# Recurrent layer of a two-model transformer kernel: output projection by tiles of the recurrence over eight sums in four PSUM banks, decay straight from the exponential, and the projection's weight splits moved behind the gates

## The chip, the cores and the metric

One core of a Trainium2 chip runs the whole kernel as one program. The metric is the device time of one execution in microseconds. Engines: TensorE (PE, with its weight loads PEld), VectorE (DVE), ScalarE (ACT), GpSimd (POOL), and SyncE (SP), which here only issues the weight transfers.

## What is computed

The first model is two layers of mixed attention over 256 tokens with 256 context tokens; its output goes through the second model: a recurrent layer, an MLP, a shared key/value projection, chunked attention and a second MLP. The change lies in the recurrent layer (width 1408 = 11 blocks of 128, model width 1024 = 8 blocks):

```python
z = hn @ w_in
gate, xr = jnp.split(z, 2, axis=-1)
xr = causal_depthwise_conv(xr, conv_w, conv_b)
r = jax.nn.sigmoid(xb @ w_a + b_a)            # by groups of 88 channels
i = jax.nn.sigmoid(xb @ w_x + b_x)
log_a = (-LRU_C * r) * jax.nn.softplus(-lam)
a = jnp.exp(log_a)
u = jnp.sqrt(-jnp.expm1(2.0 * log_a)) * (i * x)
h = scan(a, u)                                # h[t] = a[t] * h[t-1] + u[t]
x = x + gate_mod * ((h * jax.nn.gelu(gate)) @ w_out)
```

Behind it stands the norm of the MLP: the mean of the squares of x over the 1024 channels.

## The kernel before

**Numbers and layout.** All matrices are fp32, multiplied as three fp32r products of a high and a low part (`three`, lines 1678 to 1681: high by high, high by low, low by high). Activations lie with channels on the partitions and tokens in the columns.

**Units.** The weights come in 204 units, in a fixed order (`UNITS`, `PROGRAM`). Every engine walks through the same list of steps. For unit i, SyncE loads the raw weights into one of four slots (a slot is free when the unit four loads before has been split), ScalarE makes the high part (`split_hi`, L733), VectorE the low part (`split_lo`, L1054), and TensorE multiplies. As a rule both halves of unit i + 2 are made at the step of unit i, ahead of that unit's own evacuation (`evac`). The high part waits for the unit three before, whose slot it takes. For five units, `POOL_SPLIT` (63, 101, 125, 157, 173), POOL makes the low part instead (L703), because VectorE is then busy with a norm.

**The recurrent layer** is made of units 100 to 123:
- 100 to 110, `lin`: the input projection, one block of gate and of xr each. Output: `GT` (gelu of the gate) and `XR` (after the convolution).
- 111 to 116, `lgate`: the two gate matrices for two blocks each (the last for one). ScalarE evacuates: tanh of half of r (L850) and of i (L853), then `LA` = tanh of half the negative log of the decay (L859), then the decay as exponential (L863) into `T`. VectorE computes s = (a + 1) * tanh = 1 - a (L1299), bounds it (L1300), writes a = 1 - s into `LA` (L1301), and makes (i + 1) * x in `LU` (L1302) and s * (s - 2) in `XR` (L1303).
- the step `lscan`: ScalarE takes the square roots in four pieces (L1009), blocks [0, 1], [2..5], [6..9] and [10] (`LSTEPS`); VectorE multiplies a piece (L1596) and scans it block by block (L1599); POOL multiplies each scanned block by the gate (L715), which gives y; ScalarE makes the high part of y (L1012), VectorE the low part (`scan_lo`, L1492), which it does two blocks behind the scan.
- 117 to 119, `lpart`: TensorE adds blocks [0..3], [4..7] and [8..10] of y (`LPARTS`) to the four output chunks 0 to 3, which lie in two PSUM banks. Six warm-up matmuls (L1652) come first, as soon as the first block has been scanned.
- 120 to 123, `lout`: output chunks 4 to 7, one by one, each over all eleven blocks.

The high halves of units 117 and 118 stand on ScalarE ahead of the evacuations of the last two gate units, the low halves likewise on VectorE; those of 119 stand inside `lscan`.

**The norm behind it.** VectorE adds each projected chunk to x (`residual`, L1238), ScalarE squares it (L746), POOL adds the squares of chunks 1 to 6 onto that of chunk 0 one after the other (`add_squares`, L681); TensorE sums the result and the square of chunk 7 over the partitions (`sumsq`, L1900), with two warm-up matmuls behind each of the two; ScalarE takes the root, TensorE spreads it (L1909), and VectorE begins the norm's product (L1559). POOL adds the squares of unit i - 1 at the step of unit i, and its own split of unit i + 2 comes behind that:

```python
if i and fed_norm(UNITS[i - 1]) is not None:
    add_squares(UNITS[i - 1])
if i + 2 in POOL_SPLIT:
    pool.wait_ge(*at("hi", w))
    pool.tensor_tensor(wslot(wlo, w, size), ...)
```

How many chunks POOL adds is fixed by the norm, and the sum on TensorE waits for the last of them:

```python
def added(n):
    return 6 if n in (1, 3, 8) else 7
# sumsq, first part
pe.wait_ge(*at("sqadd", (n, added(n) - 1)))
```

The norm here is number 5; number 8, in the last layer, is fed by `out` units of two chunks each.

## Time and profile before

| | us |
|---|---|
| median of three runs | 1732.64 |
| the three runs | 1732.54, 1732.64, 1736.28 |
| span of the profiled execution | 1730.9 |
| time of the profiled execution as a run | not given on the page |
| TensorE busy | 1658.9 (96%) |
| VectorE busy | 1302.2 (75%) |
| ScalarE busy | 819.2 (47%) |
| POOL busy | 243.0 (14%) |

The span is from the first to the last instruction of one profiled execution. Busy times of different engines overlap. A matmul's duration is longer than the distance to the next, since matmuls are pipelined; the distance is what a matmul costs. "PEclk" is the clock granted to TensorE as a share of 2.4 GHz: 1.00 is that level, 0.50 is 1.2 GHz.

### The profile page before, as it was taken

How to read it: one execution, taken by the hardware profiler on the slowest of the kernel's cores; microseconds unless marked ns; L12 is line 12 of the kernel's file. 1: busy time of each engine (PE TensorE's matmuls, PEld its weight loads, DVE VectorE, ACT ScalarE, POOL GpSimd, SP SyncE). 2: the span in 40 equal slices, each digit the busy share in tenths (PEclk: the TensorE clock that was granted, in tenths of full speed). 3: DMA queues.
4: the chain of work that ended last, by engine and by line, in shares of the span. 5: the costliest groups of instructions: out<-in, count | busy, mean ns of one | idle time of the engine just before them, and what ended most of it. 6: DMA issues, size and time to landing. Idle time of an engine off the chain costs nothing.

```text
span 1730.9 us, 28129 instructions
## 1 busy us (share of the span) xinstructions
PE 1658.9 (96%) x11542; PEld 1464.1 (85%) x11542; DVE 1302.2 (75%) x1818; ACT 819.2 (47%) x1186; POOL 243.0 (14%) x199
## 2 busy tenths in 40 slices
PE   6999989999999999999999999969999999899999
PEld 3887768788788777986999999959999999699887
DVE  5687863887988878857578777797988868758574
ACT  3433752543133323646554546575635444555352
POOL 0423001011001111540310121013000220030000
PEclk8999999999999999999999999989999999999999
DMA  8644002243565458320347566635998966137552
GB/s 345 254 150 167 2 26 73 98 146 116 192 240 219 178 193 307 122 74 1 122 158 277 196 218 239 212 123 172 358 365 321 342 219 223 46 125 277 183 173 95
DMA packets 46575, 317.83 MB, mean 184 GB/s; under 512 B 5232, under 2 KB 6256, under 8 KB 12272
## 3 DMA queue, kind: packets, MB, share of 16 engines
q1 hardware_dynamic: 45936, 312.68, 50.0%
q0 software_dynamic: 512, 3.35, 0.5%
q8 instruction: 92, 1.51, 0.4%
q14 instruction: 35, 0.29, 0.0%
HBM read 314.96 MB, written 1.05 MB: 183 GB/s over the span
## 4 chain that ended last, share of the span: by engine, by line
PE 80%; DVE 11%; ACT 3%; issue 3%; POOL 2%; DMA 1%; SPq 0%; DVEq 0%; ACTq 0%
PE PM L1679 20%; PE PM L1680 19%; PE PM L1681 19%; PE PM L1833 5%; PE PM L1835 3%; PE PM L1963 2%; DVE wlo L1054 2%; PE PX L1999 1%; DVE acc L1088 1%; PE PX L1872 1%; PE PO L2025 1%; PE PX L1652 1%; DMA raw<-in_ada 1%; PE PO L2014 1%; PE PX L1929 1%
## 5 line engine op out<-in xcount | busy, mean ns | idle before, releaser
L1054 DVE TENSOR_TENSOR wlo<-raw,whi 128x2048 fp32r<-128x2048 f32 (+2 forms) x199 | 437.8, 2200 | 73.1 <-ACT whi L733 72.6
L1679 PE MATMUL PM<-H,whi 128*128 128x256 f32 (+1 forms) x1526 | 480.2, 315 | 7.7 <-DVE H L1480 3.0
L1680 PE MATMUL PM<-H,whi 128*128 128x256 f32 (+1 forms) x1526 | 476.2, 312 | 0.0
L1681 PE MATMUL PM<-H,wlo 128*128 128x256 f32 (+1 forms) x1526 | 476.1, 312 | 0.0
L733 ACT ACTIVATE whi<-raw 128x2048 fp32r<-128x2048 f32 (+3 forms) x204 | 365.5, 1792 | 143.2 <-PE PM L1681 48.7
L1679 PEld LDWEIGHTS PM<-H,whi 128*128 128x128 f32 x1526 | 291.1, 191 | 32.1 <-issue 7.9
L1681 PEld LDWEIGHTS PM<-H,wlo 128*128 128x128 f32 x1526 | 291.1, 191 | 16.5
L1680 PEld LDWEIGHTS PM<-H,whi 128*128 128x128 f32 x1526 | 291.3, 191 | 15.9
L1088 DVE SCALAR_TENSOR_TENSOR acc<-raw,silc,acc 128x512 f32<-128x512 f32 x328 | 245.1, 806 | 5.3 <-DMA raw<-in_ada 4.2
L1679 PE MATMUL PM<-G,whi 128*128 128x256 f32 (+1 forms) x608 | 192.7, 317 | 1.7 <-DVE X L1238 1.6
L1680 PE MATMUL PM<-G,whi 128*128 128x256 f32 (+1 forms) x608 | 190.8, 314 | 0.0
L1681 PE MATMUL PM<-G,wlo 128*128 128x256 f32 (+1 forms) x608 | 190.7, 314 | 0.0
L681 POOL TENSOR_TENSOR T<-T 128x256 f32<-128x256 f32 (+1 forms) x39 | 63.5, 1628 | 509.4 <-ACT T L746 508.8
L1679 PE MATMUL PM<-whi,H 128*128 128x256 f32 x464 | 133.2, 287 | 0.0
L1680 PE MATMUL PM<-wlo,H 128*128 128x256 f32 x464 | 131.3, 283 | 0.0
L1681 PE MATMUL PM<-whi,H 128*128 128x256 f32 x464 | 131.3, 283 | 0.0
L1679 PEld LDWEIGHTS PM<-G,whi 128*128 128x128 f32 x608 | 115.8, 191 | 13.1 <-issue 6.1
L1681 PEld LDWEIGHTS PM<-G,wlo 128*128 128x128 f32 x608 | 115.9, 191 | 7.0
L1680 PEld LDWEIGHTS PM<-G,whi 128*128 128x128 f32 x608 | 115.9, 191 | 6.6
L1238 DVE SCALAR_TENSOR_TENSOR X<-PM,mod,X 128x256 f32<-128x256 f32 x120 | 54.5, 481 | 83.5 <-issue 47.3
L622 POOL TENSOR_TENSOR T<-T 128x512 f32<-128x512 f32 (+1 forms) x44 | 48.3, 1098 | 453.9 <-DVE T L1276 453.9
L827 ACT ACTIVATE T<-PM,feat 128x512 f32<-128x512 f32 (+1 forms) x88 | 54.3, 668 | 117.1 <-PE PM L1681 108.3
(243 smaller groups left out, 2675.4 us busy)
## 6 DMA issues: line engine op xcount, KB each, us to landing
raw<-in_ada SPq DMA_DIRECT2D x104, 1024.0 KB, 5.2
raw<-in_wm SPq DMA_DIRECT2D x93, 1024.0 KB, 5.1
raw<-in_wl SPq DMA_DIRECT2D x68, 1024.0 KB, 5.1
raw<-in_wl SPq DMA_DIRECT2D x32, 704.0 KB, 4.3
raw<-in_wm SPq DMA_DIRECT2D x5, 768.0 KB, 4.5
raw<-in_wm SPq DMA_DIRECT2D x4, 704.0 KB, 4.1
X<-in_x SPq DMA_DIRECT2D x1, 2048.0 KB, 12.2
bias<-in_bias POOLq DMA_DIRECT2D x1, 2048.0 KB, 11.0
```

Of the source, the lines that this page charges most:

```text
L622: pool.tensor_tensor(g, g, val, ALU.mult).then_inc(*tick("prod", i))
L681: pool.tensor_tensor(sqslot(n, 0, W), sqslot(n, 0, W), sqslot(n, k, W), ALU.add).then_inc(*tick("sqadd", (n, k)))
L733: act.activation(wslot(whi, i, usize(u)), slot_raw(RAW_AT["w", i], usize(u)), ACT.Copy)\
L827: act.activation(dst, pm(i, part * 512, W), ACT.Identity, scale=fcol("cw", (l * 3 + 1) * 44 + n), bias=fcol("cb", l * 44 + n)).then_inc(*t ...
L1054: dve.tensor_tensor(wslot(wlo, i, usize(u)), slot_raw(n, usize(u)), wslot(whi, i, usize(u)).bitcast(F32), ALU.subtract)\
L1088: ins = dve.scalar_tensor_tensor(out=dst, in0=w, scalar=s, in1=dst, op0=ALU.mult, op1=ALU.add)
L1238: ins = dve.scalar_tensor_tensor(out=dst, in0=pm(i, m * each + who * 256, 256), scalar=modc(v, who, c), in1=dst, op0=ALU.mult, op1=ALU.add)
L1679: pe.matmul(out, st_hi, mv_hi, start=first, stop=False)
L1680: pe.matmul(out, st_hi, mv_lo, start=False, stop=False)
L1681: return pe.matmul(out, st_lo, mv_hi, start=False, stop=last)
L1833: pe.matmul(pm(i, c * 512, 512), wslot(whi, i, 128, w0), mh[:, k * 512:k * 512 + 512], start=(k == 0), stop=False)
L1835: ins = pe.matmul(pm(i, c * 512, 256), wslot(wlo, i, 128, w0), mh[:, k * S:k * S + 256], start=False, stop=(k == kt - 1))
```

## The change

1. The projection. `lpart` units 117 to 119 now hold two blocks of y each, [0, 1], [2, 3], [4, 5], for all eight output chunks; the eight sums lie in four PSUM banks (`lsum`). Units 120 to 123 are now `lend`: blocks 6 to 10 for two output chunks each. Each `lend` unit feeds the norm with two chunks.
2. The decay. ScalarE writes the exponential straight into `LA` and the tanh into `T`; VectorE's instruction that wrote 1 - s into `LA` is gone.
3. The splits. Unit 117 is split behind the evacuation of the fifth gate unit, 118 no longer at the sixth but in `lscan` behind block 1, 119 behind block 3 and 120 behind block 6.
4. The scan. Its pieces are [0], [1, 2], [3..6], [7..10], and the low part of y is made one block behind the scan, not two.

```diff
-LPARTS = [[0, 1, 2, 3], [4, 5, 6, 7], [8, 9, 10]]
-LSTEPS = [[0, 1], [2, 3, 4, 5], [6, 7, 8, 9], [10]]
+LPARTS = [[0, 1], [2, 3], [4, 5]]
+LEND = [6, 7, 8, 9, 10]
+LSTEPS = [[0], [1, 2], [3, 4, 5, 6], [7, 8, 9, 10]]
...
-        add("lpart", "M0", n, len(ks), 512, 256)
-    for n in range(4, KD):
-        add("lout", "M0", n, NL, 128, 256)
+        add("lpart", "M0", n, len(ks), 1024, 256)
+    for n in range(KD // 2):
+        add("lend", "M0", n, len(LEND), 256, 256)
...
 def chunks_of(u):
 
-    if u["kind"] == "out":
+    if u["kind"] in ("out", "lend"):
         return [2 * u["idx"], 2 * u["idx"] + 1]
...
+        def lsum(c):
+
+            return PM[:, c // 4, c % 4 * 256:c % 4 * 256 + 256]
+
+        def lsplit_at(u):
+
+            if u["kind"] == "lgate" and u["idx"] >= len(GATE_UNITS) - 2:
+                return "late" if u["idx"] == len(GATE_UNITS) - 2 else None
+            return None if u["kind"] == "lpart" and u["idx"] < 2 else "first"
+
+        LSPLIT = {1: first_of("lpart", "M0") + 1, 3: first_of("lpart", "M0") + 2, 6: first_of("lend", "M0")}
...
-                        ins = act.activation(LA[:, j * 256:j * 256 + 256], rs[:, c * 256:c * 256 + 256], ACT.Tanh, scale=lcol(6, j), bias=lcol(6, j))
+                        ins = act.activation(LA[:, j * 256:j * 256 + 256], rs[:, c * 256:c * 256 + 256], ACT.Exp, scale=lcol(7, j), bias=lcol(7, j))
...
-                        ins = act.activation(rs[:, c * 256:c * 256 + 256], rs[:, c * 256:c * 256 + 256], ACT.Exp, scale=lcol(7, j), bias=lcol(7, j))
+                        ins = act.activation(rs[:, c * 256:c * 256 + 256], rs[:, c * 256:c * 256 + 256], ACT.Tanh, scale=lcol(6, j), bias=lcol(6, j))
...
-                        if j == 2:
-                            split_hi(first_of("lpart", "M0") + 2)
+                        if j in LSPLIT:
+                            split_hi(LSPLIT[j])
...
-                    dve.tensor_scalar(th, s, -1.0, 1.0, ALU.mult, ALU.add).then_inc(*C.link("dve_chain"))
...
-                            if j >= 2:
-                                scan_lo(j - 2)
-                            if j == 5:
-                                split_lo(first_of("lpart", "M0") + 2)
-                    scan_lo(NL - 2)
+                            if j >= 1:
+                                scan_lo(j - 1)
+                            if j - 1 in LSPLIT:
+                                split_lo(LSPLIT[j - 1])
...
-                        for c in range(4):
-                            w0 = m * 512 + c * 128
-                            ins = three(pm(first_of("lpart", "M0"), c * 256, 256), wslot(whi, i, 128, w0), wslot(wlo, i, 128, w0),
-                                        mh[:, k * 256:k * 256 + 256], ml[:, k * 256:k * 256 + 256], k == 0 and c % 2 == 0, k == NL - 1 and c % 2 == 1)
+                        for c in range(KD):
+                            w0 = m * 1024 + c * 128
+                            ins = three(lsum(c), wslot(whi, i, 128, w0), wslot(wlo, i, 128, w0),
+                                        mh[:, k * 256:k * 256 + 256], ml[:, k * 256:k * 256 + 256], k == 0 and c % 2 == 0, False)
+                elif kind == "lend":
+                    for c in range(2):
+                        for m, k in enumerate(LEND):
+                            if c == 0:
+                                pe.wait_ge(*at("hlo", ("y", k)))
+                            w0 = m * 256 + c * 128
+                            ins = three(lsum(2 * u["idx"] + c), wslot(whi, i, 128, w0), wslot(wlo, i, 128, w0),
+                                        mh[:, k * 256:k * 256 + 256], ml[:, k * 256:k * 256 + 256], False, k == NL - 1 and c == 1)
```

`added` and `POOL_SPLIT` are as before. How the instructions stand on three engines (each row: line, operation, output and inputs, shape, the semaphores that it waits for, and how often in a row):

POOL, from the gate multiplications of the scan to the norm behind the projection and on. Before:

```order
L715 TENSOR_TENSOR LU<-XR,GT 128x256 [waits s_lh] x11
L681 TENSOR_TENSOR T<-T 128x256 [waits s_sq]
L681 TENSOR_TENSOR T<-T 128x256 [waits s_sq,s_sqadd] x5
L703 TENSOR_TENSOR wlo<-raw,whi 128x2048 [waits s_hi]
L681 TENSOR_TENSOR T<-T 128x256 [waits s_sq]
```

Now:

```order
L724 TENSOR_TENSOR LU<-XR,GT 128x256 [waits s_lh] x11
L690 TENSOR_TENSOR T<-T 128x256 [waits s_sq]
L690 TENSOR_TENSOR T<-T 128x256 [waits s_sq,s_sqadd] x4
L712 TENSOR_TENSOR wlo<-raw,whi 128x2048 [waits s_hi]
L690 TENSOR_TENSOR T<-T 128x256 [waits s_sq,s_sqadd]
```

The addition of chunk 6 stood ahead of the split of unit 125 and stands behind it now.

ScalarE, from the end of the fifth gate unit (111 + 4) to the roots. Before:

```order
L863 ACTIVATE T<-T,lk 128x256 [waits s_act_chain]
L863 ACTIVATE T<-T,lk 128x256
L733 ACTIVATE whi<-raw 128x2048 [waits s_unit,s_raw2]
L850 ACTIVATE T<-PM,lk 128x256 [waits s_la,s_prep,s_unit,s_hi]
L853 ACTIVATE LU<-PM,lk 128x256
L859 ACTIVATE LA<-T,lk 128x256 [waits s_pm_act]
L863 ACTIVATE T<-T,lk 128x256 [waits s_act_chain]
L1009 ACT_TABLE_LOAD
L1009 ACTIVATE XR<-XR 128x512 [waits s_la]
L1009 ACTIVATE XR<-XR 128x1024 [waits s_la] x2
```

Now:

```order
L872 ACTIVATE T<-T,lk 128x256 [waits s_act_chain]
L872 ACTIVATE T<-T,lk 128x256
L742 ACTIVATE whi<-raw 128x2048 [waits s_unit,s_raw1]
L859 ACTIVATE T<-PM,lk 128x256 [waits s_la,s_prep,s_unit,s_hi]
L862 ACTIVATE LU<-PM,lk 128x256
L868 ACTIVATE LA<-T,lk 128x256 [waits s_pm_act]
L872 ACTIVATE T<-T,lk 128x256 [waits s_act_chain]
L1018 ACT_TABLE_LOAD
L1018 ACTIVATE XR<-XR 128x256 [waits s_la]
L1018 ACTIVATE XR<-XR 128x512 [waits s_la]
L1018 ACTIVATE XR<-XR 128x1024 [waits s_la] x2
```

The split that stands between the two gate units is now that of 117 (slot raw1), which stood one unit further ahead; that of 118 (raw2) is gone from here.

VectorE, in the scan, from the multiplication of the second piece. Before:

```order
L1596 TENSOR_TENSOR LU<-LU,XR 128x1024 [waits s_ls]
L1599 SCALAR_TENSOR_TENSOR XR<-LA,LU 128x256 [waits s_dve_chain]
L1492 TENSOR_TENSOR H_54<-LU,H_54 128x256 [waits s_hhi]
L1599 SCALAR_TENSOR_TENSOR XR<-LA,LU 128x256
L1492 TENSOR_TENSOR H_54<-LU,H_54 128x256 [waits s_hhi]
```

Now:

```order
L1606 TENSOR_TENSOR LU<-LU,XR 128x512 [waits s_ls]
L1609 SCALAR_TENSOR_TENSOR XR<-LA,LU 128x256 [waits s_dve_chain]
L1502 TENSOR_TENSOR H_54<-LU,H_54 128x256 [waits s_hhi]
L1609 SCALAR_TENSOR_TENSOR XR<-LA,LU 128x256
L1502 TENSOR_TENSOR H_54<-LU,H_54 128x256 [waits s_hhi]
L1065 TENSOR_TENSOR wlo<-raw,whi 128x2048 [waits s_hi]
L1606 TENSOR_TENSOR LU<-LU,XR 128x1024 [waits s_ls]
```

A split of 2048 columns, waiting for ScalarE's half, has come in between the second piece and the third; a second one stands after two more blocks, and one of 1280 columns after block 7.

## Rows read from the trace of the kernel before

**Rows 1.** The page: parts 1 and 6, TensorE's share, and the transfers of 1024 KB.

```profile
PE 1658.9 (96%) x11542; PEld 1464.1 (85%) x11542; DVE 1302.2 (75%) x1818; ACT 819.2 (47%) x1186; POOL 243.0 (14%) x199
...
raw<-in_wm SPq DMA_DIRECT2D x93, 1024.0 KB, 5.1
```

**Rows 2.** Time by stage: stretch, length, busy us of each engine (instructions), clock, DMA share, GB/s.

```profile
1141.00:1154.00 13.00, 0.39 (x4) 0.18 (x2) 12.10 (x19) 12.73 (x19) 0.00 (x0) 0.60 0.42 145
1154.00:1174.00 20.00, 18.36 (x115) 16.97 (x116) 19.79 (x25) 5.79 (x12) 10.15 (x11) 0.83 0.13 45
1174.00:1194.00 20.00, 20.00 (x169) 20.00 (x168) 12.70 (x14) 12.04 (x15) 8.72 (x7) 1.00 0.66 219
...
1205.00:1390.00 185.00, 184.70 (x1586) 179.69 (x1585) 160.10 (x194) 92.60 (x93) 12.36 (x6) 1.00 0.89 336
```

**Rows 3.** ScalarE in order of time: start us, us, what, shapes, count [idle before].

```profile
1140.13 1.90 ACT L733 ACTIVATE whi<-raw 128x2048 fp32r<-128x2048 f32 x1
1142.06 0.84 ACT L850 ACTIVATE T<-PM,lk 128x256 f32<-128x256 f32 x2
...
1144.78 1.09 ACT L863 ACTIVATE T<-T,lk 128x256 f32<-128x256 f32 x2
1145.78 1.89 ACT L733 ACTIVATE whi<-raw 128x2048 fp32r<-128x2048 f32 x1
```

**Rows 4.** VectorE in order of time, from the last split before the scan to its end.

```profile
1148.84 2.28 DVE L1054 TENSOR_TENSOR wlo<-raw,whi 128x2048 fp32r<-128x2048 f32 x1
...
1153.66 1.27 DVE L1599 TENSOR_TENSOR_SCAN XR<-LA,LU 128x256 f32<-128x256 f32 x2
...
1159.04 0.39 DVE L1492 TENSOR_TENSOR H<-LU,H 128x256 fp32r<-128x256 f32 x1
1159.35 1.21 DVE L1599 TENSOR_TENSOR_SCAN XR<-LA,LU 128x256 f32<-128x256 f32 x1
...
1162.27 2.29 DVE L1054 TENSOR_TENSOR wlo<-raw,whi 128x1536 fp32r<-128x1536 f32 x1
...
1174.10 0.42 DVE L1492 TENSOR_TENSOR H<-LU,H 128x256 fp32r<-128x256 f32 x1 [0.20 <-ACT H L1012]
```

**Rows 5.** POOL in order of time: one gate multiplication in the scan.

```profile
1159.19 0.82 POOL L715 TENSOR_TENSOR LU<-XR,GT 128x256 f32<-128x256 f32 x1 [0.63 <-DVE XR L1599]
```

**Rows 6.** TensorE in order of time: the warm-up at the scan, and the norm's sum.

```profile
1154.61 5.46 PE L1652 MATMUL PX<-cst 128*128 128x256 f32 x12 [13.22 <-DVE XR L1599]
1159.51 0.78 PE L1679 MATMUL PM<-H,whi 128*128 128x256 f32 x1
...
1193.41 0.51 PE L1900 MATMUL PO<-cst,T 128*128 128x2 f32 x4
1193.77 1.11 PE L1652 MATMUL PX<-cst 128*128 128x256 f32 x4
1194.72 0.54 PE L1900 MATMUL PO<-cst,T 128*128 128x2 f32 x4
```

**Rows 7.** VectorE: residual behind unit 122, and the first product of norm 5.

```profile
1189.70 0.48 DVE L1238 SCALAR_TENSOR_TENSOR X<-PM,mod,X 128x256 f32<-128x256 f32 x1 [1.94 <-issue]
...
1196.71 0.48 DVE L1559 SCALAR_TENSOR_TENSOR T<-X,mod,PO 128x256 f32<-128x256 f32 x1 [0.95 <-PE PO L1909]
```

**Rows 8.** VectorE's residual of two chunks in the last layer, then POOL's adds and split.

```profile
1532.74 0.88 DVE L1238 SCALAR_TENSOR_TENSOR X<-PM,mod,X 128x256 f32<-128x256 f32 x2 [2.69 <-issue]
...
1533.87 3.36 POOL L681 TENSOR_TENSOR T<-T 128x256 f32<-128x256 f32 x2 [2.40 <-ACT T L746]
1537.18 4.55 POOL L703 TENSOR_TENSOR wlo<-raw,whi 128x2048 fp32r<-128x2048 f32 x1
```

**Rows 9.** TensorE by the microsecond: stretch, length, busy us (instructions), granted clock, DMA share, GB/s.

```profile
1141.00:1142.00 1.00, 0.39 (x4) 1.00 0.80 298
...
1143.00:1144.00 1.00, 0.00 (x0) 0.83 0.03 11
1144.00:1145.00 1.00, 0.00 (x0) 0.50 0.00 0
```

More of the change, by code:

```diff
@@ L214, in fed_norm @@
     n = FEEDS.get((u["kind"], u["st"]))
-    if u["kind"] == "lpart" and u["idx"] < len(LPARTS) - 1:
-        return None
     if n is None or u["idx"] < FIRST_HALF.get(u["kind"], 0):
@@ L265 @@
 COLUMNS_AT = [ROWS_AT[i - 1] if i else [] for i in range(NU)]
-POOL_SPLIT = [u["i"] + 2 for u in UNITS if (fed_norm(u) or 0) >= 3 and chunks_of(u)[-1] == KD - 1 and u["kind"] != "lpart"]
+POOL_SPLIT = [u["i"] + 2 for u in UNITS if (fed_norm(u) or 0) >= 3 and chunks_of(u)[-1] == KD - 1]
 def raw_order():
@@ L1020, in _ @@
                         ffn_stage2(UNITS[i - 1])
-                    if (u["kind"], u["idx"]) != ("lpart", 0):
+                    if lsplit_at(u) == "first":
                         split_hi(i + 2)
@@ L1025, in _ @@
                     evac(u)
+                    if lsplit_at(u) == "late":
+                        split_hi(i + 2)
                     for hv in DIRECT_AT[i]:
@@ L1057, in chunk_soon @@
             def chunk_soon(u):
-                return (fed_norm(u) or 0) >= 3 and u["kind"] != "lpart" and (u["kind"] != "down" or u["idx"] % KD > 0)
+                return (fed_norm(u) or 0) >= 3 and (u["kind"] != "down" or u["idx"] % KD > 0)
             marks = [None, None]
@@ L1224, in residual @@
                 st = u["st"]
-                v = vec_base(st) + (2 if u["kind"] in ("out", "lout", "lpart") else 5)
+                v = vec_base(st) + (2 if u["kind"] in ("out", "lend") else 5)
                 n = fed_norm(u)
@@ L1230, in residual @@
                 cs = chunks_of(u)
-                each = 256 if u["kind"] == "lpart" else 512
                 for m, c in enumerate(cs):
@@ L1262, in evac @@
                     dve.tensor_tensor(v4, v4, r4, ALU.mult).then_inc(*tick("avn", i))
-                elif kind in ("out", "down", "lout", "w2") or (kind, u["idx"]) == ("lpart", len(LPARTS) - 1):
+                elif kind in ("out", "down", "lend", "w2"):
                     residual(u)
@@ L1609, in _ @@
                     soon = chunk_soon(u)
-                    if (u["kind"], u["idx"]) != ("lpart", 0) and not soon and not (u["kind"] == "w1" and wide(u)):
+                    if lsplit_at(u) == "first" and not soon and not (u["kind"] == "w1" and wide(u)):
                         split_lo(i + 2)
@@ L1616, in _ @@
                     evac(u)
-                    if soon:
+                    if soon or lsplit_at(u) == "late":
                         split_lo(i + 2)
@@ L1657, in pm_free @@
             def pm_free(i):
-                if i >= 2 and not (UNITS[i]["kind"] == "lpart" and UNITS[i]["idx"]):
+                if i >= 2 and UNITS[i]["kind"] != "lend" and not (UNITS[i]["kind"] == "lpart" and UNITS[i]["idx"]):
                     u = UNITS[i - 2]
@@ L1669, in pm_free @@
                         pe.wait_ge(*at("vcopy", i - 2))
-                    if u["kind"] in ("out", "down", "lout", "w2") or (u["kind"], u["idx"]) == ("lpart", len(LPARTS) - 1):
+                    if u["kind"] in ("out", "down", "lend", "w2"):
                         n = fed_norm(u)
@@ L1786, in unit @@
                 pm_free(i)
-                if kind == "lpart" or (kind == "lout" and UNITS[i - 1]["kind"] == "lpart"):
+                if (kind, u["idx"]) == ("lpart", 0):
                     pe.wait_ge(*at("pm_act", first_of("lpart", "M0") - 1))
```

15 lines of the change are left out of this document (7 added, 8 removed).

## The prediction

> **What bounds the kernel now.** I read the page's first part, then the time by stage, then each engine's instructions in the stretch that the change touches. TensorE is busy for 96% of the span [rows 1], so most stages end with its last matmul, and work taken off another engine is worth something only where TensorE waits for it. One such place lies in the recurrent layer. From 1141 to 1154 us TensorE is busy for 0.39 us of 13, while ScalarE and VectorE are busy for 12.73 and 12.10; right behind it, TensorE works at a mean granted clock of 0.83; from 1174 on it is busy without a gap at 20.00/169 = 0.12 us a matmul, and it stays so from 1205 to 1390 [rows 2]. So the stretch is: gates, decay and scan on ScalarE and VectorE, then the projection on TensorE, then the fifth norm, whose first matmul (the sum of squares) starts at 1193.41 and whose first product on VectorE starts at 1196.71 [rows 6, 7]. What comes later is bound by TensorE and passes on what it is given: in 185 us it has 0.3 us of idle time that could take up a shift. The sum is therefore the move of that 1196.71.
>
> **The gates and the decay.** ScalarE's order is split 117 (1.90 us), gate unit 4 (from 1142.06 to 1144.78 + 1.09 = 1145.87), split 118 (1.89), gate unit 5, table load, square roots [rows 3]. The change puts split 117 behind gate unit 4 and takes split 118 out of the stretch: the roots start 1.9 us earlier. VectorE loses its half of split 118 here (2.28 us [rows 4]), and the first multiplication ahead of the scan is of 256 columns, not 512: at 2.28/2048 columns that is 0.3 us. The instruction dropped per gate unit (1 - s) lies on VectorE in time that it mostly waits for ScalarE; swapping exponential and tanh costs ScalarE nothing, since one table load of each kind stays. I take 2.6 us in all: the first scan starts at 1153.66 - 2.6 = 1151.05.
>
> **The scan chain.** In the steady part VectorE and POOL take turns. The scan that is issued at 1159.35 ends at 1160.56, though a scan takes 0.6 us alone (two in 1.27); it ends 0.55 us after the POOL multiplication that ran from 1159.19 to 1160.01. The low part of y (1159.04 to 1159.43) does run under that POOL instruction, and a block costs 1.45 us [rows 4, 5]. The Trainium skill (SBUF - State Buffer, "SBUF: two separate sides") says that the shared port pair is held for the whole of an instruction and the loser fully blocks. By that the low part could not lie under it, a block would cost about 0.3 us more, ten of them 3 us, and the sum below would be 9.6 instead of 6.6; the row decides, for the same instructions.
>
> From first scan to last low part it is now 1153.66 to 1174.52, 20.9 us [rows 4]. The change takes out the split of 1536 columns (2.3) and puts in two of 2048 (2 x 2.28) and one of 1280 (1.4 by its columns, plus 0.6 behind a POOL instruction). VectorE has the first two at once behind a low part, but ScalarE makes their other half only behind its copy of the same y block: 0.42 + 1.90 from the end of POOL's product, against 0.55 + 0.3 for scan and low part, so VectorE waits some 1.4 us, twice. The last multiplication of 256 columns between blocks goes (0.9 with its wait for POOL). 20.9 - 2.3 + 4.6 + 2.0 + 2.8 - 0.9 = 27.1, and the last low part is done at 1151.05 + 27.1 = 1178.2, 3.6 us later than now.
>
> **The projection.** The 264 matmuls stay 264; before, 12 per block of y lie under the scan and 132 behind it, now 24 for each of the first six blocks and 120 in the four end units. The six warm-up matmuls start 0.95 us after the first scan and take 4.9 [rows 6]; useful work starts at 1156.9. With 0.7 lost on its first, slow matmuls, TensorE alone would be through at 1156.9 + 0.7 + 264 x 0.12 = 1189.3. But it comes to block 8 at 1175.6 and has to wait for blocks 9 and 10. The weights are the same 5632 KB in seven transfers; a slot is free for the next one when VectorE's split of the unit four loads before is done, so those of the last two end units are asked for at about 1159 and 1166, land in some 5 us [rows 1], and ScalarE wants them after 1179: no wait. Behind the last low part stand 3 + 15 + 90 = 108 matmuls: 1178.2 + 0.15 + 13.0 = 1191.35. Before, the last one gave way at 1193.41. This part gains 2.1 us.
>
> **The norm behind it, where I see the loss.** POOL executes in order. Before, chunk 6 was added at the step of its unit and POOL's own split of unit 125 came after it. Now chunks 6 and 7 come from one unit, POOL adds 4 and 5, splits unit 125, and only then adds 6; TensorE's first sum of squares waits for that addition, with the warm-up and everything of the norm queued behind it. The same order, adds 4 and 5 and then a split, is to be seen in the last layer: residual of two chunks at 1532.74, the adds held behind VectorE's split (3.36 us for two), POOL's split from 1537.18 for 4.55, so it is through 9.0 us after the residual began [rows 8]. Here that residual follows the third end unit at 1191.35 - 30 x 0.12 + 0.09 (as at 1189.70 now [rows 7]) = 1187.85. Split through at 1196.85, add 6 (0.82 [rows 5]) at 1197.65, sum of squares at 1197.75. TensorE is idle for 6.4 us. Against 1193.41 that is +4.3 us.
>
> **The clock.** When TensorE went idle at 1141.4 the granted clock was still 1.00 in the first microsecond, 0.83 in the third and 0.50, the 1.2 GHz level, from the fourth [rows 9]. A wait of 6.4 us is longer than that, so the norm's matmuls should run at 1.2 GHz. Price: four records of warm-up take 0.95 us at full clock (1193.77 to 1194.72), twelve took 4.90 at half, 0.24 and 0.41 each; eight of them 1.4 more. The small matmuls around them, 0.36 us ahead of the first warm-up and twice about as much later, 1.2 in all, at the same ratio of 1.7 give 0.9 more [rows 6]. Bounds: nothing, if the clock holds or comes back at once, and 3.3, if the whole of 1193.41 to 1196.71 doubles. I take 2.3, nearest to the rows.
>
> Sum: +4.3 + 2.3 = **+6.6 us**, in parts -2.1 (projection ends earlier), +6.4 (wait), +2.3 (clock). On the profiled execution the span goes from 1730.9 to 1737.5. The page gives no time of its own for that execution; the fastest run, 1732.54, is 1.6 us above the span and the median 0.1 above that. I add to the median: **1739.2 us**. Of the 4 us by which the third run stood higher nothing shows in the trace. A difference of 0.3%, 5.2 us, is about what a measurement can tell from none.
>
> **Rivals.**
> A, the clock holds through the wait: +4.3, 1736.9, which is not slower by 0.3%. For it: after 1141.4 it held for some 2 us. Against: it fell in that gap, the one long gap in these rows. It decides if TensorE waits hardly longer than those 2 us, or does something in between. 0.10.
> B, also not slower by 0.3%: the scan chain does not hold the projection. Place: VectorE's two waits for ScalarE's halves and block 10. If block 10 is done by 1176, the projection ends with TensorE at 1189.3, 2.1 us earlier, and the sum is +4.5, 1737.1. Against: two splits of 2.28 us stand in the chain whatever the waits are. 0.12.
> C, the addition is not late, so the change does not stall the norm: it needs POOL's split to be through when square 6 is, at 1192.4. Then 1191.35 + 0.1 + 0.5 + 0.5 + 0.8 + 0.1 = 1193.35 and the sum is -0.1, 1732.5. Against: the split takes 4.55 and its input, ScalarE's half, is not made before unit 122 ends. 0.08.
> D, four banks: each block of y goes round eight sums in four banks instead of four in two. If that pulled the clock to 1.2 GHz, 144 matmuls would cost 0.08 more each (ratio 1.7): 12, less the 2 us of slack, so +17, 1749. For the two banks of now the clock is 1.00 from 1174. 0.05. The Trainium skill (TensorE: Matmul & The Clock Gate, "A second HAM failure mode: psum-queue depth-cycling") tells of a kernel where cycling through banks made the clock oscillate; by that rule this case decides.
> E, faster by over 5.2 us: the whole bound of the gain is 4.1 us with no wait in the norm, so something outside the stretch would have to help. 0.05.
>
> **The numbers.** The forecast has 0.60, with a range of its own from +5.2 to +8.5 (a clock price between 1 and 3, the chain within 1 us). Faster by over 0.3%: E, 0.05. Within: A, B and C, 0.30. Slower: forecast and D, 0.65. The range goes from 1735.0 to 1742.5: it takes in the forecast, A and B with a microsecond or two of their spread and leaves out C, D and E, 0.18.
>
> **What would show it.** In the changed profile: first scan near 1151; two gaps of some 1.4 us on VectorE ahead of its splits in the scan; TensorE waiting for low parts near 1177; the last projection matmul near 1191; then a wait of TensorE of 6.4 us for POOL's addition, and a granted clock of 0.5 behind it. Wrong would be a first sum of squares before 1195, POOL's addition 6 ahead of its split, or an idle stretch in the norm stage with the clock still at 1.00.

## The result, and the profile of the changed kernel

The changed kernel is slower: its median of six runs is 1741.1 us (1739.24 to 1749.78) beside 1734.76 us of six runs of the kernel before (1732.54 to 1736.28). The ratio of the two is 1.0051, with a 95% interval from 1.0033 to 1.0070, so 0.3% to 0.7% slower, or 6 to 12 us. The profiled execution of the changed kernel has a span of 1737.4 us and was a run of 1739.24.

The span alone misleads here. It is 6.5 us longer than that of before, the medians stand 6.3 apart, and 6.6 was the forecast, but they agree by accident. To see it, follow one row that both kernels have: the reciprocal in norm 4, ahead of the recurrent layer (DVE, start, duration), first of the kernel before, then of the changed one.

```profile
1046.58 0.17 DVE L1537 RECIPROCAL rcol<-rcol 128x2 f32<-128x2 f32 x1 [1.44 <-ACT rcol L974]
```

```profile
1045.96 0.17 DVE L1547 RECIPROCAL rcol<-rcol 128x2 f32<-128x2 f32 x1 [1.62 <-ACT rcol L983]
```

The changed kernel comes 0.6 us early to the stretch. That is no work of the change: in the fourteen traces of this case the row stands anywhere from 1043.74 to 1052.47. Norm 5's first product starts at 1205.60 instead of 1196.71 [rows 7], 8.9 us later:

```profile
1205.60 0.87 DVE L1569 SCALAR_TENSOR_TENSOR T<-X,mod,PO 128x256 f32<-128x256 f32 x2 [2.31 <-PE PO L1926]
```

From norm 4's reciprocal to that product it is 159.64 us against 150.13: **the change costs 9.5 us**, and the missing 3 us of the span are 0.6 ahead of the stretch and 2.4 in the last MLP, which the last section shows. Comparisons of traces below use such distances within one trace, since whole executions of one kernel differ by more than the terms in question (the 29 to 34 runs of the kernel before in each of the three groups of experiments spread over 10 us and more).

Time by stage of the changed kernel, to be held against [rows 2] (stretch, length, then busy us of TensorE, its weight loads, VectorE, ScalarE and POOL with their instructions, granted clock, DMA share, GB/s):

```profile
1154.00:1174.00 20.00, 19.96 (x155) 19.37 (x155) 17.18 (x20) 7.31 (x10) 5.64 (x7) 0.97 0.23 70
1174.00:1194.00 20.00, 16.36 (x117) 15.55 (x116) 13.15 (x17) 11.46 (x16) 9.32 (x9) 0.91 0.61 213
1205.00:1390.00 185.00, 184.70 (x1572) 179.20 (x1572) 161.08 (x204) 94.06 (x98) 8.66 (x4) 1.00 0.85 325
```

TensorE is fed under the scan, from 1154 to 1174, as the change sets out to do: 155 matmuls instead of 115. Behind that it has gaps and a lower clock. What it waits for, from 1110 to 1215 us (sum, times, longest):

```profile
PE PX L1661 <- DVE XR L1609: 11.0, 1, 11.0
PE PO L1917 <- POOL T L690: 6.2, 1, 6.2
...
PE PM L1688 <- DVE H L1502: 2.6, 3, 0.9
```

The first wait is the one of 13.2 us ahead of the scan, now 2.2 shorter. The second is new: the norm's sum waits for POOL's addition. The third, three waits for low parts of y, was there in another form. VectorE in the scan (start, duration, idle before):

```profile
1150.46 0.69 DVE L1609 TENSOR_TENSOR_SCAN XR<-LA,LU 128x256 f32<-128x256 f32 x1
1151.07 0.67 DVE L1606 TENSOR_TENSOR LU<-LU,XR 128x512 f32<-128x512 f32 x1
...
1156.09 2.29 DVE L1065 TENSOR_TENSOR wlo<-raw,whi 128x2048 fp32r<-128x2048 f32 x1 [1.38 <-ACT whi L742]
...
1163.44 2.29 DVE L1065 TENSOR_TENSOR wlo<-raw,whi 128x2048 fp32r<-128x2048 f32 x1 [1.38 <-ACT whi L742]
...
1170.80 2.03 DVE L1065 TENSOR_TENSOR wlo<-raw,whi 128x1280 fp32r<-128x1280 f32 x1
...
1175.16 1.22 DVE L1609 TENSOR_TENSOR_SCAN XR<-LA,LU 128x256 f32<-128x256 f32 x1
...
1177.82 0.43 DVE L1502 TENSOR_TENSOR H<-LU,H 128x256 fp32r<-128x256 f32 x1 [1.07 <-ACT H L1021]
```

The two gaps of 1.38 us and the two long splits are as forecast. So is the third split's 2.03 (the same shape takes 1.49 at 1179.27, with nothing on POOL, so beginning under a POOL instruction cost 0.54). The gap of 1.07 ahead of the last low part, where 0.20 stood before [rows 4], was not. POOL and VectorE at the end of the projection:

```profile
1190.63 3.34 POOL L690 TENSOR_TENSOR T<-T 128x256 f32<-128x256 f32 x2 [1.03 <-ACT T L755]
1193.92 4.50 POOL L712 TENSOR_TENSOR wlo<-raw,whi 128x2048 fp32r<-128x2048 f32 x1
1198.38 0.73 POOL L690 TENSOR_TENSOR T<-T 128x256 f32<-128x256 f32 x1
```

```profile
1193.10 0.88 DVE L1249 SCALAR_TENSOR_TENSOR X<-PM,mod,X 128x256 f32<-128x256 f32 x2 [0.52 <-DVE wlo L1065]
```

Chunk 6 is ready for POOL from 1194 on and is added at 1198.38, behind the split. TensorE in the norm, against [rows 6]:

```profile
1199.25 0.99 PE L1917 MATMUL PO<-cst,T 128*128 128x2 f32 x4 [6.25 <-POOL T L690]
1200.10 2.05 PE L1661 MATMUL PX<-cst 128*128 128x256 f32 x4
1201.94 0.85 PE L1917 MATMUL PO<-cst,T 128*128 128x2 f32 x4
```

Last, TensorE by the microsecond (busy us, granted clock, DMA share, GB/s):

```profile
1176.00:1177.00 1.00, 0.20 (x1) 1.00 0.95 401
1177.00:1178.00 1.00, 0.41 (x3) 1.00 0.02 8
1178.00:1179.00 1.00, 0.70 (x6) 1.00 0.00 0
1179.00:1180.00 1.00, 1.00 (x8) 0.58 0.00 0
1180.00:1181.00 1.00, 1.00 (x7) 0.50 0.00 0
...
1195.00:1196.00 1.00, 0.00 (x0) 1.00 1.02 434
1196.00:1197.00 1.00, 0.00 (x0) 0.61 0.69 287
1197.00:1198.00 1.00, 0.00 (x0) 0.50 0.00 0
```

The clock falls to 1.2 GHz twice: in the wait of 6.25 us, as forecast, and already at 1179, in the first end unit, which no step of the prediction had.

### The profile page after: what moved, and what is told of

Same layout as the page of the kernel before. It is cut to its first block, busy times and chain, and to the rows that moved or that the text cites. A ratio compares the mean times of both kernels' runs of the same rounds, so it can differ in the third digit from the quotient of the medians.

```text
span 1737.4 us, 28124 instructions
## 1 busy us (share of the span) xinstructions
PE 1657.9 (95%) x11542; PEld 1463.1 (84%) x11542; DVE 1299.0 (75%) x1812; ACT 819.4 (47%) x1186; POOL 243.3 (14%) x199
## 3 DMA queue, kind: packets, MB, share of 16 engines
HBM read 314.96 MB, written 1.05 MB: 182 GB/s over the span
## 4 chain that ended last, share of the span: by engine, by line
PE 78%; DVE 11%; ACT 4%; issue 3%; POOL 2%; DMA 1%; SPq 0%; DVEq 0%; ACTq 0%; POOLq 0%
PE PM L1688 19%; PE PM L1689 19%; PE PM L1690 19%; PE PM L1850 5%; PE PM L1852 3%; DVE wlo L1065 2%; PE PM L1980 2%; PE PX L2016 1%; DVE acc L1099 1%; PE PX L1889 1%; PE PO L2042 1%; PE PO L2031 1%; DMA raw<-in_ada 1%; PE PX L1946 1%; ACT whi L742 1%
## 5 line engine op out<-in xcount | busy, mean ns | idle before, releaser
L1065 DVE TENSOR_TENSOR wlo<-raw,whi 128x2048 fp32r<-128x2048 f32 (+3 forms) x199 | 437.6, 2199 | 76.8 <-ACT whi L742 76.3
L742 ACT ACTIVATE whi<-raw 128x2048 fp32r<-128x2048 f32 (+4 forms) x204 | 365.5, 1792 | 142.6 <-PE PM L1690 52.1
```

The costliest lines, as they stand in the source:

```text
L742: act.activation(wslot(whi, i, usize(u)), slot_raw(RAW_AT["w", i], usize(u)), ACT.Copy)\
L1065: dve.tensor_tensor(wslot(wlo, i, usize(u)), slot_raw(n, usize(u)), wslot(whi, i, usize(u)).bitcast(F32), ALU.subtract)\
```

## The experiments

Four rows of each trace carry the comparison: the first scan, the last residual of the projection, the norm's first sum on TensorE, and the norm's first product. The table gives the start of the first scan behind norm 4's reciprocal, the other three behind the first scan, and the whole distance, less the 150.13 us of the kernel before. A number in brackets is the profiled trace's first scan, for finding the rows. The ratios given with the medians compare each version with the runs of the kernel before in its own group.

| kernel | first scan behind norm 4 | last residual | first sum | first product | whole, against before |
|---|---|---|---|---|---|
| before (1153.66) | 107.08 | 40.00 | 39.75 | 43.05 | 0 |
| changed (1150.46) | 104.50 | 42.64 | 48.79 | 55.14 | +9.51 |
| e1_sum67 (1148.25) | 104.51 | 42.61 | 43.63 | 48.65 | +3.03 |
| e7_pool_first (1154.54) | 104.50 | 42.65 | 44.60 | 50.59 | +4.96 |
| e2_warm_wait (1155.77) | 104.49 | 41.50 | 47.67 | 52.01 | +6.37 |
| e5_warm_lend (1156.17) | 104.51 | 41.49 | 47.64 | 53.47 | +7.85 |
| e3_split_later (1151.48) | 104.50 | 39.62 | 45.77 | 52.11 | +6.48 |
| e6_both (1155.36) | 104.50 | 39.63 | 40.65 | 44.44 | -1.19 |
| e8_fill (1156.97) | 104.50 | 39.77 | 40.79 | 44.58 | -1.05 |
| e12_both_again (1155.52) | 104.49 | 39.62 | 40.63 | 45.53 | -0.11 |
| e4_decay_alone (1155.39) | 106.56 | 40.00 | 39.74 | 43.05 | -0.52 |
| e9_before_splits (1151.50) | 105.30 | 42.19 | 41.93 | 45.24 | +0.41 |
| e10_changed_again (1153.10) | 104.50 | 42.64 | 48.79 | 55.14 | +9.51 |
| e11_before_again (1154.36) | 107.09 | 39.99 | 39.74 | 43.04 | 0.00 |

**e1_sum67: is it the addition of chunk 6?**

```diff
-            return 6 if n in (1, 3, 8) else 7
+            return 6 if n in (1, 3, 5, 8) else 7
```

> The changed kernel, but POOL adds chunks 1 to 5 only in norm 5, and TensorE sums the squares of 6 and 7 itself. Theory (the addition of chunk 6 behind POOL's own split costs 6.2 us of TensorE and the clock behind it 3.1): the first sum of squares starts at about 1194.1 instead of 1199.25, the clock stays at 1.00, and the norm's first product starts at about 1197.8 instead of 1205.60: 7.8 us faster than the changed kernel, about 1 us slower to level with the kernel before. Rival 1 (the addition is only what the wait is booked on; POOL's split or ScalarE's squares are late whoever adds): the wait stays above 3 us with another name, gain under 4. Rival 2 (the loss is the projection's): gain 3 at most.

Median 1735.68 us of 12 runs, 1.0007 of before (0.9994 to 1.0019). The wait is 1.1 us, and what is left of it is POOL's addition of chunk 5:

```profile
1191.88 0.58 PE L1917 MATMUL PO<-cst,T 128*128 128x2 f32 x4 [1.11 <-POOL T L690]
...
1193.27 0.95 PE L1917 MATMUL PO<-cst,T 128*128 128x2 f32 x8
1194.08 1.94 PE L1661 MATMUL PX<-cst 128*128 128x256 f32 x4
```

The first sum comes 5.16 us earlier, as expected (5.15). The first product gains 6.5, not 7.8: the clock, expected to stay up, fell all the same, now inside the norm, and the second warm-up took 1.94 us instead of 1.11. Rivals 1 and 2 both fall: the gain is far above 3 or 4.

**e7_pool_first: is it the order on POOL alone?** The number of additions stays at seven; POOL's split of unit 125 goes one step later.

```diff
-                    if i + 2 in POOL_SPLIT:
-                        w = i + 2
+                    w = i + 1 if i + 1 == 125 else i + 2
+                    if w in POOL_SPLIT and (i, w) != (123, 125):
```

> The changed kernel, POOL still adding chunk 6, but its split of unit 125 one step later, behind that addition. Theory (the order of two instructions on POOL is the whole wait): square 6 done 0.95 us behind the last residual's start, addition 0.8, first sum at 1.9 behind it instead of 6.15; TensorE idle for 2.1 us instead of 6.25, clock perhaps held; first product 5.2 (held) to 7 us (fallen) behind the last residual instead of 12.5: 5.5 to 7.3 us faster than the changed kernel. Rival (unit 125's low part is then too late for TensorE): a new wait at unit 125 takes back some of it.

Median 1738.32 us of 12 runs, 1.0027 of before (1.0015 to 1.0039). POOL:

```profile
1198.27 0.72 POOL L690 TENSOR_TENSOR T<-T 128x256 f32<-128x256 f32 x1 [0.20 <-ACT T L755]
1198.95 4.51 POOL L712 TENSOR_TENSOR wlo<-raw,whi 128x2048 fp32r<-128x2048 f32 x1
```

First sum 1.95 us behind the last residual instead of 6.15, 4.55 us gained up to the product, with the clock at 0.50 in the norm. That is 0.95 below the range given: the fallen clock makes the distance from residual to product 7.94, not 7. Nothing waits for the later split: TensorE has no wait between 1206 and 1250. So two instructions on POOL in the wrong order were 4.2 of the 6.25 us; the 2.04 that are left are chunk 6's own residual, square and addition.

**e2_warm_wait: what is the clock worth?**

```diff
                     if step[0] == "norm" and late:
+                        warm(("wait", step[1]), 12 if step[1] == 5 else 0)
```

> The changed kernel with twelve warm-up matmuls (0.475 us each at full clock, 5.7 in all) ahead of norm 5's first sum of squares, inside TensorE's wait of 6.25 us for POOL; nothing that it waits for is moved. Theory (the 3.1 us that the norm takes longer than before are the clock alone): the first sum stays at 1199.2, the granted clock stays at 1.00, and the first product starts 3.3 us later, at 1202.5: 3.1 us faster than the changed kernel. Rival (the norm is longer because something else in it is late, ScalarE's root or a transfer): clock 1.00 and first product still near 1205; no gain.

Median 1739.2 us of 10 runs, 1.0035 of before (1.0023 to 1.0047). The whole gains 3.1 us, the expected number, but not where it was expected. The clock did not fall in the projection of this run (last residual at 41.50 instead of 42.64: 1.1 us), and from first sum to first product it took 4.34 us instead of 6.35 (2.0), since the clock held through the filled wait and fell only 2 us into the norm (0.79 in the microsecond from 1205, 0.50 behind it). The expectation had 3.3 for this, the time of the kernel before. So that the clock lengthens the norm is shown; the sum of 3.1 is a coincidence of two parts.

**e5_warm_lend: idle time or the four banks?**

```diff
                             if c == 0:
+                                if u["idx"] == 0 and k >= 8:
+                                    warm(("low", k), 2)
                                 pe.wait_ge(*at("hlo", ("y", k)))
```

> The changed kernel with two warm-up matmuls (0.95 us) inside each of TensorE's three waits of 0.88 us for the low parts of blocks 8, 9 and 10. Theory (the clock falls behind 1178 because TensorE is mostly idle for 4 us, and this costs 1.1 us: the last residual stands 42.64 us behind the first scan in the changed kernel and 41.50 in the run in which the clock held): the clock stays at 1.00 through the projection, the last residual stands at 41.5 to 41.7 behind the first scan. Rival (going round eight sums in four banks makes the clock fall, idle or not): it falls again, distance 42.6 or more.

Median 1742.0 us of 4 runs, 1.0054 of before (1.0036 to 1.0072). TensorE where the waits were:

```profile
1180.00:1182.00 2.00, 1.98 (x12) 1.00 0.83 348
1182.00:1184.00 2.00, 1.98 (x11) 1.00 0.28 119
1184.00:1186.00 2.00, 2.00 (x16) 1.00 0.00 0
```

Clock 1.00 throughout the projection, last residual at 41.49, as expected. This alone doesn't decide between idle time and banks, because e2_warm_wait held the clock without any fill. What speaks against the banks is where the clock stood: at 1.00 from 1156 to 1173 in the changed kernel, where the 144 matmuls go round eight sums in four banks, and at 0.5 behind 1179, in a unit that stays in one bank. The Trainium skill (TensorE: Matmul & The Clock Gate, "A second HAM failure mode: psum-queue depth-cycling") tells of a kernel in which such cycling made the clock oscillate, through short idle times between the groups of matmuls. In this kernel the trace has no idle time between them, and no oscillation in any of the ten traces with this projection.

**e3_split_later: does the scan chain hold the projection?**

```diff
-                            if j - 1 in LSPLIT:
-                                split_lo(LSPLIT[j - 1])
+                            if j - 2 in LSPLIT:
+                                split_lo(LSPLIT[j - 2])
```

> The changed kernel, VectorE's three splits inside the scan one block later each, so that ScalarE's half is ready. Theory (the scan chain holds the projection, and its two waits of 1.38 us are the whole difference to what it could be): both gaps go, the last low part is done at about 1175.5 instead of 1178.25, TensorE's three waits of 0.88 us mostly go and with them the fall of the clock at 1179; the projection ends at about 1188.5 instead of 1192.9, and since the addition of chunk 6 follows the third end unit's residual, all behind it comes 4.3 us earlier: 4.3 us faster than the changed kernel. Rival 1 (TensorE is already the bound by then, or the waits go elsewhere, to low parts delayed by the split): gain under 1.5. Rival 2 (clock falls at 1179 whatever the waits, from going round four banks): gain 2.8, clock still 0.5 in a stretch behind 1174.

Median 1739.83 us of 12 runs, 1.0028 of before (1.0014 to 1.0041). Both gaps are gone:

```profile
1158.37 2.83 DVE L1065 TENSOR_TENSOR wlo<-raw,whi 128x2048 fp32r<-128x2048 f32 x1
...
1163.54 2.83 DVE L1065 TENSOR_TENSOR wlo<-raw,whi 128x2048 fp32r<-128x2048 f32 x1
...
1176.95 0.43 DVE L1502 TENSOR_TENSOR H<-LU,H 128x256 fp32r<-128x256 f32 x1 [1.07 <-ACT H L1021]
```

The last low part starts 25.47 us behind the first scan instead of 27.36: 1.9 gained, not 2.8. Each of the two large splits now begins under one of POOL's gate products (1158.22 to 1159.05 for the first) and takes 2.83 instead of 2.29. The last residual gains 3.0, of which 1.9 is the chain and 1.1 the clock, which held. 4.3 was expected. The chain was to give 2.8 of that; the 0.9 missing there is the balance of what now runs beside POOL (0.54 more on each of the two splits, and a multiplication of 1024 columns at 1.75 where it took 1.22) and the scans that no longer do. The other 1.5 was left for the clock, where the runs show 1.1. The chain does hold the projection, and rival 2, the banks, falls: the clock is 1.00 up to the norm, with two waits of TensorE for low parts left (0.76 and 0.87 us).

**e6_both and e12_both_again: do the two add up?** The edits of e1 and e3 together.

> Edits of e1_sum67 and e3_split_later together. Theory (two separate terms that add up): first scan to last residual 39.6 as in e3_split_later, last residual to first product 4.3 to 6.0 as in e1_sum67 with the clock held or not; from first scan to first product 44 to 45.6 us against 55.14 in the changed kernel and 43.05 in the one before, whose first scan is 2.6 us later: 0 to 1.7 us faster than before, 9.5 to 11 faster than the changed kernel. Rival (POOL's split, which starts behind addition 5, or ScalarE now holds the norm): distance above 47.

> e6_both once more, beside the changed kernel on the same chip. From the traces: 1.2 us faster than before, 10.7 us faster than the changed kernel (first scan to first product 44.44 against 55.14). Rival: the clock falls in this run at blocks 8 to 10 or in the norm, which would take 1 to 1.5 us each and leave it level with before.

Medians 1732.46 us of 12 runs, 0.9994 of before (0.9984 to 1.0005), and 1731.57 of 12, 0.9998 (0.9984 to 1.0012). In the group of e12_both_again the changed kernel had 1742.22, so this version is 10.7 us faster than that, and level with the kernel before as far as these runs can tell. From first scan to first product it is 44.44 us in e6_both, within the 44 to 45.6 expected, and 45.53 in e12_both_again, where the rival came true. Over the whole distance that is 1.2 us ahead of the kernel before in one trace and 0.1 in the other, with the same rows up to the sum. The difference is the clock in the norm. First e6_both, then e12_both_again:

```profile
1198.20 1.11 PE L1661 MATMUL PX<-cst 128*128 128x256 f32 x4
1199.15 0.61 PE L1926 MATMUL PO<-cst,rcol 128*128 128x128 f32 x4
```

```profile
1198.35 1.81 PE L1661 MATMUL PX<-cst 128*128 128x256 f32 x4
1199.95 1.06 PE L1926 MATMUL PO<-cst,rcol 128*128 128x128 f32 x4
```

**e8_fill: can the clock be held?** e6_both with two warm-up matmuls ahead of each of the waits for blocks 8 to 10 and two ahead of the norm's sum.

> e6_both with two warm-up matmuls ahead of each of the waits for blocks 8 to 10 and two ahead of norm 5's first sum. Theory (what is left to gain is the clock): granted clock 1.00 from first low part to the norm's product, last residual to first product 4.3 us, 43.9 from first scan to first product: 1.7 us faster than before in the trace. Rival (the clock holds in e6_both anyway, or falls in spite of the fill): the same as e6_both within 0.5.

Median 1733.78 us of 12 runs, 0.9995 of before (0.9986 to 1.0005). The clock held, as it did in e6_both without them, and the distance is 44.58 us, not the 43.9 expected: the rival of the two was right, and the fill costs 0.14 us (last residual at 39.77). Whether it prevents the fall of e12_both_again would take many traces: not settled.

**e4_decay_alone.** The kernel before with the second part of the change.

```diff
-                    dve.tensor_scalar(th, s, -1.0, 1.0, ALU.mult, ALU.add).then_inc(*C.link("dve_chain"))
```

(and the exponential and the tanh of ScalarE exchanged, as in the change)

> The kernel before with the second part of the change alone: the exponential straight into the decay, no 1 - s on VectorE. Theory (that instruction lies in time in which VectorE waits for ScalarE): first scan within 0.3 us of 1153.66 counted from the end of the gates, the same time within 0.5 us. Rival (VectorE's chain behind the last gate unit is on the path): first scan up to 0.9 us earlier (two instructions of 0.29 to 0.5) and the kernel 0.3 to 0.9 us faster.

Median 1733.34 us of 11 runs, 1.0 of before (0.9989 to 1.0012). First scan 0.52 us earlier: the rival was right. What is dropped in the fourth gate unit only lengthens VectorE's wait ahead of the fifth, from 0.52 to 0.85 us; the fifth starts 99.41 us behind norm 4 where it started 99.40. Behind that wait there is none, and the instructions dropped in the fifth and sixth (0.34 and 0.21 us of VectorE's time, from start to next start) are the gain.

**e9_before_splits.** The kernel before with the third part alone.

```diff
-                        if j == 2:
-                            split_hi(first_of("lpart", "M0") + 2)
+                        if j in (1, 3):
+                            split_hi(first_of("lpart", "M0") + 1 + j // 2)
...
-                            if j == 5:
-                                split_lo(first_of("lpart", "M0") + 2)
+                            if j in (3, 6):
+                                split_lo(first_of("lpart", "M0") + j // 3)
```

(and no split of 118 at the gates, that of 117 behind the fifth unit's evacuation)

> The kernel before with the third part of the change alone: split 117 behind the fifth gate unit's evacuation, split 118 inside the scan (ScalarE behind block 1, VectorE behind the scan of block 3), 119 one block later; projection and decay as before. Theory (the split only changes its place in a chain that VectorE bounds; it pays only together with the new projection, which has fewer matmuls behind the last low part): first scan 1.8 us earlier than the 1153.66 of before (the 2.6 less 0.5 for the decay and 0.3 for the first multiplication), the chain 2.3 to 2.8 us longer, so the norm's first product 0.5 to 1.0 us later than before. Rival (the splits alone are the gain and the new projection adds nothing): first product more than 1 us earlier than before.

Median 1733.99 us of 10 runs, 0.9997 of before (0.9982 to 1.0012). First scan 1.78 us earlier, first product 0.41 later. The moved split of 2048 columns is in the chain (2.78 us, begun under a POOL product), which grows by 2.2:

```profile
1157.24 2.78 DVE L1062 TENSOR_TENSOR wlo<-raw,whi 128x2048 fp32r<-128x2048 f32 x1
```

So parts two and three of the change bring an earlier scan of 2.3 us, and only the first can pay for the longer chain, by leaving 108 matmuls behind the last low part where there were 144 (12 of block 10 and 132 of the four other chunks).

**e10_changed_again and e11_before_again.**

> The changed kernel once more. Three runs with its projection (after, e1_sum67, e7_pool_first) showed the clock at 0.5 for 3 us behind the waits for blocks 8 to 10, one with the same instructions there (e2_warm_wait) did not. If the fall is a matter of chance: either value here, last residual 42.6 or 41.5 us behind the first scan; the 0.5 behind the wait of 6.25 us again in any case, first product 55.1 or 54.0 behind the first scan. If it is fixed by the kernel: 42.64 and 55.14 again. In the last MLP the units of TensorE stand 5.65 us apart in the kernel before and 5.545 in the changed one: if that belongs to the kernel it is 5.545 again throughout.

> The kernel before once more, as the other half of the same question. First scan to first product 43.05 us again. In the last MLP: 5.65 us a unit again if the distance belongs to the kernel, otherwise it may be 5.545, or change within the run as in e6_both.

Medians 1742.22 us of 6 runs, 1.0052 of before (1.0034 to 1.0070), and 1734.73 of 8, 1.0007 (0.9992 to 1.0021). Every distance of the table comes back within 0.02 us, the 9.51 too. The clock fell in the projection again. In the five traces with the changed kernel's own instructions there (the changed kernel twice, e1_sum67, e7_pool_first, e2_warm_wait) it fell four times and held once, in e2_warm_wait.

## Why the prediction was right and where it fell short

The sign and the main cause were right: slower by more than 0.3%, and the wait of TensorE for POOL's addition where it was announced. The size was 6.6 us and is 9.5, because two terms of the sum failed: the projection, forecast to gain 2.1 us, gains nothing, and the clock in the norm, forecast at 2.3, costs 3.05. That 1741.1 us lies within 1735.0 to 1742.5, and near the 1739.2 forecast, is in part luck: the forecast was added to 1732.64, the median of three runs, where six runs give 1734.76, and the medians differ by 6.3 us where the traces show 9.5 for the change. The medians, with their interval of 6 to 12 us, could not have told the failed terms. Step by step:

- **First scan.** Forecast 2.6 us earlier; measured 2.58 (107.08 to 104.50). The parts were not quite what I had said. The dropped 1 - s was costed at nothing because VectorE mostly waits there; e4_decay_alone gives it 0.52.
- **Scan chain.** Forecast 27.1 us from the first scan to the end of the last low part, 6.2 more than before; measured 1150.46 to 1178.25, 27.8, 6.9 more. By VectorE's rows, from start to next start, the terms are: splits +4.16 (forecast 4.3), the two waits 2.76 (2.8), multiplications -0.20 (-0.9), the wait ahead of the last low part +0.88 (0), scans and low parts -0.67 (0). Two things were missing. The prediction took out the multiplication of 256 columns between blocks and did not put in that of 512 columns, 0.70 us at 1151.07, which the new pieces bring. And it read the fourth part of the change, the low part one block behind the scan and not two, as free. Its price is less than the new wait of 1.07 us: the low part that filled this time before now stands ahead of the last scan, where it takes 0.34, and from the end of the last scan to the start of the last low part it is 1.44 us instead of 1.39. That makes 0.4; no run varies this order alone. The last scan of before, to be held against 1175.16 above:

```profile
1172.02 0.69 DVE L1599 TENSOR_TENSOR_SCAN XR<-LA,LU 128x256 f32<-128x256 f32 x1
```

- **The row under POOL.** The prediction took a low part from 1159.04 to 1159.43 as running under POOL's product. It starts 0.15 us ahead of that product, so the row does not show what a low part costs that starts behind one. The 9.6 us that the prediction works out for the other case stand close to the 9.5 measured by chance: a block of y still costs 1.49 us (1173.67 to 1175.16) where it cost 1.45, not 0.3 more.
- **"This part gains 2.1 us"** is the step that failed. In the trace the projection gains nothing: the last residual comes at 104.50 + 42.64 = 147.14 behind norm 4, and before at 107.08 + 40.00 = 147.08. Of the 2.2 us between forecast and measurement, 0.7 is the chain, and 1.1 is the clock, 42.64 against 41.50 and 41.49 in the runs where it held. Most of the rest stands in the trace of e2_warm_wait: the second end unit starts at 1186.12, 0.26 behind the end of the first, just behind VectorE's low half of its weights, ready at 1184.57 + 1.49 = 1186.06:

```profile
1184.57 1.49 DVE L1065 TENSOR_TENSOR wlo<-raw,whi 128x1280 fp32r<-128x1280 f32 x1 [1.03 <-ACT whi L742]
```

```profile
1186.12 0.39 PE L1688 MATMUL PM<-H,whi 128*128 128x256 f32 x1
```

I had checked that these weights land in time, not that they are split in time. In the changed kernel's own trace the slow matmuls of the first end unit hide this.
- **The clock there.** The prediction weighed a fall in the projection only for the banks (rival D, 0.05). The cause that fits the rows is another: TensorE works 0.6 us and waits 0.88, three times in a row, from 1174 to 1178 (busy for 0.20, 0.41 and 0.70 us in the last three of these microseconds). The "three waits" were in the prediction as time lost and not as a threat to the clock. With the waits filled (e5_warm_lend), and with two of them left in place of three (e3_split_later, e6_both), it did not fall; since it also held once with all three (e2_warm_wait), these few traces make the cause likely and do not prove it. The Trainium skill (TensorE: Matmul & The Clock Gate, "HAM oscillation — how this bites in real kernels") tells of a kernel whose clock falls anew in each wait for a transfer, waits of about 3 to 5 us. The waits here are 0.88 us each, so it does not foretell this fall; these rows show one behind shorter waits, four times of five.
- **The wait in the norm.** Forecast 6.4 us, measured 6.25. The model for it, the same order of adds and a split in the last layer [rows 8], carried over to 0.15 us: 9.0 from residual to the split's end there, 1198.42 - 1189.50 = 8.9 here. This is what e1_sum67 and e7_pool_first confirm: take the addition away or put it first, and 5.1 or 4.2 us of the wait go.
- **The clock in the norm.** Forecast 2.3 us, with 3.3 as the upper bound "if the whole of 1193.41 to 1196.71 doubles"; measured 1205.60 - 1199.25 = 6.35 against 3.30, so 3.05. It nearly doubles. I had priced only the matmuls that I saw; the ones in the chain from sum to root and back slow down as well (the four that spread the root went from 0.61 us in e6_both to 1.06 with the clock down in e12_both_again).

Sum of what failed: 2.2 in the projection and 0.75 in the norm, less 0.15 in the wait: 2.8 of the 2.9 us missing.

Of the rivals, A (clock holds) and C (addition not late) are refuted by the changed kernel's own rows, D by the clock of 1.00 from 1156 to 1173, and E by the result. B is refuted too: it said that the chain does not hold the projection, but TensorE waits for the low parts of blocks 8 to 10, and e3_split_later, with a chain 1.9 us shorter, ends the projection that much earlier besides what the clock gives.

## What to carry over

When work is regrouped so that one unit delivers two results where two units delivered one each, look at every engine that executes in order and had something between the two: here a split of 4.5 us slid in front of an addition of 0.7, and the engine that waits for the addition had its whole norm behind it. A wait that is forecast is also a question to the clock; price what follows it at 1.2 GHz in full, matmul by matmul of the whole chain, and count several short waits in a row as a threat to it too (here three of them, four times of five). And compare two traces by distances between rows that both have, not by their spans: here the spans agreed with the forecast to 0.1 us while two terms of the sum were wrong.

## What the runs showed of the hardware

**TensorE ran one instruction sequence at two steady rates.** In the last MLP, where a matmul of 512 columns and one of 256 alternate, the units stand 5.65 or 5.545 us apart, at a granted clock of 1.00. The kernel before has 5.65 throughout in its profiled run, the changed one 5.545 (VectorE's residuals, first two of before, then two of after):

```profile
1619.80 0.48 DVE L1235 SCALAR_TENSOR_TENSOR X<-PM,mod,X 128x256 f32<-128x256 f32 x1 [1.32 <-PE PM L1835]
1625.44 0.48 DVE L1235 SCALAR_TENSOR_TENSOR X<-PM,mod,X 128x256 f32<-128x256 f32 x1 [1.31 <-PE PM L1835]
```

```profile
1611.63 0.48 DVE L1245 SCALAR_TENSOR_TENSOR X<-PM,mod,X 128x256 f32<-128x256 f32 x1 [1.09 <-PE PM L1852]
1617.18 0.48 DVE L1245 SCALAR_TENSOR_TENSOR X<-PM,mod,X 128x256 f32<-128x256 f32 x1 [1.21 <-PE PM L1852]
```

That is the 2.4 us by which the changed kernel's span looks better. It does not belong to the kernel: e10_changed_again and e11_before_again, the same two kernels, change from one rate to the other in the middle of the stage, and so does e6_both:

```profile
1633.53 0.48 DVE L1245 SCALAR_TENSOR_TENSOR X<-PM,mod,X 128x256 f32<-128x256 f32 x1 [1.21 <-PE PM L1852]
1639.08 0.48 DVE L1245 SCALAR_TENSOR_TENSOR X<-PM,mod,X 128x256 f32<-128x256 f32 x1 [1.21 <-PE PM L1852]
...
1700.80 0.48 DVE L1245 SCALAR_TENSOR_TENSOR X<-PM,mod,X 128x256 f32<-128x256 f32 x1 [1.38 <-PE PM L1852]
1706.45 0.48 DVE L1245 SCALAR_TENSOR_TENSOR X<-PM,mod,X 128x256 f32<-128x256 f32 x1 [1.38 <-PE PM L1852]
```

What sets it was not tried.

**The fall of the clock behind short waits is not fixed by the instructions.** The same instructions with the same waits of 0.88 us kept it in e2_warm_wait and lost it in four other traces; behind a single wait of 1.11 us it held in e6_both and fell in e12_both_again and e1_sum67. Behind the waits of 6.24 or 6.25 us it fell in all four traces that have one unfilled (the changed kernel twice, e3_split_later, e5_warm_lend).
